# Position bias and causal mask of the softmax heads: added by VectorE, in place of a product on TensorE

## The chip, the cores and the metric

The kernel runs on one core of one Trainium2 chip. The metric is the device time of one execution in microseconds (us). The kernel before has a median of 721.65 us over 3 runs (721.18 to 724.95).

## What is computed

The reference is one layer of a decoder trunk, run for a prompt of 512 tokens and for 8 short samples of 4 tokens with a cache of 256. One input projection feeds three groups of heads: 6 softmax heads with a linear position bias (ALiBi), 6 stick-breaking heads, and a gated MLP over chunks. An output projection, a layer norm, an MLP of width 4096 and a second layer norm follow. The change touches the softmax heads of the prompt alone. Cut to that:

```python
s = jnp.einsum('bhqd,bhnsd->bhqns', qc, kg).astype(jnp.float32) * scale
dist = (pc[:, None, None] - kpos).astype(jnp.float32)
s = s - slopes[:, None, None, None] * dist
mask = ok[..., None] & (kpos <= pc[:, None, None])
s = jnp.where(mask, s, -jnp.inf)
p = jax.nn.softmax(s.reshape(Bn, H, qb, ns * MOBA_BLOCK), axis=-1)
...
return jnp.einsum('bhqns,bhqnsd->bhqd', p, vg)
```

With 512 tokens, key blocks of 256 and three blocks to choose, every past block is chosen, so that this is plain causal softmax attention with a bias of slope times (key position minus query position).

## The kernel before, in words

The kernel is written engine by engine. Each engine has its own program in a fixed order, and semaphores join them: `pe.wait_ge(x, n)` holds everything behind it on TensorE until semaphore `x` has reached `n`. Nothing is scheduled by a planner.

**Products in three passes.** An fp32 matrix is split into a high and a low part in the type fp32r (`w_hi`, `w_lo`, `h_hi`, `h_lo`), and each product is done as high by high, low by high, high by low. All such products stand on line 1510. The input projection has 22 units of 128 output columns. A unit is cut into 8 chunks of 6 matmuls each (`in_unit(u, c)`); chunks 0 to 3 are 256 columns wide and chunks 4 to 7 are 288.

**The attention loop.** The two kinds of prompt heads are handled as 48 items: item n is head pair i = n // 8, query block t = (n % 8) // 2 and head h = n % 2, with L = 128 (t + 1) keys. Items 0 to 23 are softmax heads, 24 to 47 are stick-breaking heads. So L is 128, 128, 256, 256, 384, 384, 512, 512 through the 8 items of a pair. The chunks of units 3 to 21 are woven in. TensorE does in step n: `scores(n)`, a chunk, `turn_probs(n - 2)`, a chunk, at every fourth step `values`, in the first three steps of a pair `turn_kv`, and a third chunk.

- `scores(n)` (lines 1541 to 1563) writes one of the two score banks `s_bank` in PSUM. For a softmax item it is three accumulated matmuls of L columns: the bias and mask (L1557: the scaled identity `sid_r` by the table of distances `dist_r`, which holds -1e30 beyond the diagonal), and two for query by key (L1558, L1559). It first waits until the bank is free (`p_written`, n - 1).
- `row_max(n)` on VectorE (L1114, L1116): the maximum of each row of the bank, then its negative, `nmx`.
- `probs(n)` on ScalarE (L788): exp of the bank with `nmx` as bias and the row sum as a second output, into `prob`.
- `normalise(n - 1)` on VectorE (L1123, L1125) comes behind `row_max(n)` in VectorE's order: `prob` times the inverse row sum. It releases `p_scaled`.
- `turn_probs(n)` on TensorE (L1572) waits for `p_scaled` and transposes `prob`.

VectorE and ScalarE carry more work in the same fixed order. VectorE (lines 1144 to 1169): in step s = n % 8 behind `normalise`, a copy `kv_new` (s = 2, L1155), the low part of the finished head pair `m_lo` (s = 3, L1159), half of each projected unit (`read_half`, s = 2, 5, 7, L1080, L1082), and the low parts of the stacked queries and keys of the next pair (`stack_q_lo`, s = 0 and 4, L1092; `stack_k_lo`, s = 6, L1099). ScalarE (lines 800 to 834) does the other halves, the high parts of these stacks (L756, L763), the copies of keys and values `k_tok` and `v_tok` (L810), the high part of the finished pair (L817), and `w_hi` of the next weights (L692). So a query stack goes ScalarE, then VectorE, and what stands behind it on VectorE waits for both.

**GpSimd** computes the low parts of all weights (L582), and early on writes `dist_r` (L599), the six scaled identities `sid_r` (L601), `id_r` and `below_r` (L603, L604). TensorE waits for all nine (`bias_ready`, H + 3) before item 0.

Of the kernel before, what the change touches and what calls it, by code (L numbers as in the profile page):

```python
# [27 lines left out]
ALU = mybir.AluOpType  # L28
ACT = mybir.ActivationFunctionType
AX_X = mybir.AxisListType.X  # L30
F32 = mybir.dt.float32
F32R = mybir.dt.float32r
I32 = mybir.dt.int32

P = 128
D_MODEL = 1024
KT = D_MODEL // P
SEQ = 512
# [9 lines left out]
H = 6  # L48
PAIRS = H // 2
# [14 lines left out]
SLOPES = [0.25, 0.0625, 0.015625, 0.00390625, 0.5, 0.125]  # L64
# [40 lines left out]
def hybrid_layer(nc, x_prompt, x_sample, weights, cache_k_a, cache_v_a, cache_k_b, cache_v_b,  # L105
# [14 lines left out]
    with ExitStack() as ctx:  # L120
        def sb(name, shape, dt=F32, to=None):
            return (to or ctx).enter_context(nc.sbuf_tensor(name, shape, dt))

        def sem(name):
            return ctx.enter_context(nc.semaphore(name))
# [13 lines left out]
        warm = sb("warm", [P, 1])  # L139
        qbd = [sb(f"qbd{y}", [P, NB, PAIRS, 32]) for y in range(2)]  # L140
        dist_r = sb("dist_r", [P, SEQ], F32R)
        sid_r = sb("sid_r", [P, H, P], F32R)
        id_r = sb("id_r", [P, P], F32R)
        below_r = sb("below_r", [P, P], F32R)

# [29 lines left out]
        prob = sb("prob", [P, 3, SEQ], to=pr)  # L175
        prob_t = [sb(f"prob_t{h}", [P, QT * (QT + 1) // 2, P], to=pr) for h in range(2)]
        mx = sb("mx", [P, 2], to=pr)
        nmx = sb("nmx", [P, 2], to=pr)
# [4 lines left out]
        keep = sb("keep", [P, 2, SEQ], to=pr)  # L183
# [57 lines left out]
        def c_(name, r=P, lo=0, hi=None):  # L241
            where, t = (CONST, cst) if name in CONST else (S_CONST, s_cst)
            at, n = where[name]
            if t is s_cst and at < S_ROWS:
                t = s_rows
            elif t is s_cst:
                at -= S_ROWS
            return t[0:r, at + lo:at + (n if hi is None else hi)]
# [35 lines left out]
        kv_out = [sem(f"kv_out{j}") for j in range(2)]  # L284
        s_ready = sem("s_ready")
        row_maxed, max_ready = sem("row_maxed"), sem("max_ready")
        p_written = sem("p_written")
        rsum_inverted = sem("rsum_inverted")
        stick_left = sem("stick_left")
# [287 lines left out]
        def _(pool):  # L577
# [19 lines left out]
            lo_part(2, 2 % STAGE, 2)  # L597
            pool.wait_ge(const2_loaded, 32)
            pool.tensor_copy(dist_r[:, :], dist[:, :]).then_inc(bias_ready, 1)  # L599
            for h in range(H):  # L600
                pool.tensor_scalar(sid_r[:, h, :], c_("ident"), SLOPES[h], None, ALU.mult).then_inc(bias_ready, 1)  # L601
            lo_part(3, 3 % STAGE, 3)
            pool.tensor_copy(id_r[:, :], c_("ident")).then_inc(bias_ready, 1)  # L603
            pool.tensor_copy(below_r[:, :], c_("below_neg")).then_inc(bias_ready, 1)  # L604
# [82 lines left out]
        def _(act):  # L687
# [87 lines left out]
            def probs(n):  # L775

                i, s, t, h, L = item(n)
                b = n % 2
                if i < PAIRS:
                    act.wait_ge(max_ready, n + 1)  # L780
                else:
                    act.wait_ge(s_ready, n + 1)
                    act.wait_ge(p_scaled, n - 1)
                    act.activation(keep[:, b, 0:L], s_bank[b][:, 0:L], ACT.Sigmoid, scale=-1.0)
                if n >= 3:
                    act.wait_ge(pt_ready, n - 2)
                if i < PAIRS:
                    act.activation(prob[:, n % 3, 0:L], s_bank[b][:, 0:L], ACT.Exp, bias=nmx[:, b:b + 1],  # L788
                                   accum_out=rsum[:, b:b + 1]).then_inc(p_written, 1)
                else:  # L790
                    act.activation(prob[:, n % 3, 0:L], s_bank[b][:, 0:L], ACT.Sigmoid).then_inc(p_written, 1)
# [8 lines left out]
            for n in range(ITEMS + 4):  # L800
                i, s = divmod(n, 8)
# [221 lines left out]
        def _(dve):  # L1023
# [85 lines left out]
            def row_max(n):  # L1109

                i, s, t, h, L = item(n)
                b = n % 2
                dve.wait_ge(s_ready, n + 1)
                dve.tensor_reduce(mx[:, b:b + 1], s_bank[b][:, 0:L], AX_X, ALU.max).then_inc(row_maxed, 1)  # L1114
                dve.wait_ge(row_maxed, n + 1)
                dve.tensor_scalar(nmx[:, b:b + 1], mx[:, b:b + 1], -1.0, None, ALU.mult).then_inc(max_ready, 1)  # L1116

# [23 lines left out]
                                  ALU.mult).then_inc(p_scaled, 1)  # L1141

            dve.wait_ge(const2_loaded, 32)
            for n in range(ITEMS + 4):
                i, s = divmod(n, 8)
                if n < 8 * PAIRS:
                    row_max(n)
                if 1 <= n <= 8 * PAIRS:
                    normalise(n - 1)
                elif 8 * PAIRS < n <= ITEMS:  # L1150
                    stick(n - 1)
                if n < ITEMS and s == 2:
                    y, p = divmod(i, PAIRS)
                    dve.wait_ge(kv_turned, 3 * i + 3)
                    dve.tensor_copy(kv_new[y][:, :, P * p:P * (p + 1)],  # L1155
                                    acc[0:NS, 3, 0:2 * P].rearrange("t (w c) -> t w c", w=2)).then_inc(kv_new_ready, 1)
                if i >= 1 and s == 3:
                    dve.wait_ge(mhi_ready, i)
                    dve.scalar_tensor_tensor(m_lo[:, i - 1, PROMPT], o_bank[:, :], 1 / ALPHA,  # L1159
                                             m_hi[:, i - 1, PROMPT].bitcast(F32), ALU.mult,  # L1160
                                             ALU.subtract).then_inc(m_ready, 1)
                if i and n < ITEMS and s == 0:
                    stack_q_lo(i, 1)
                if n < ITEMS and s in (2, 5, 7):
                    read_half(3 * (i + 1) + (2, 5, 7).index(s))
                if i + 1 < 2 * PAIRS and s == 4:
                    stack_q_lo(i + 1, 0)
                if i + 1 < 2 * PAIRS and s == 6:
                    stack_k_lo(i + 1)
# [309 lines left out]
        def _(pe):  # L1479
# [50 lines left out]
            for u in range(3):  # L1530
                for c in range(8):
# [4 lines left out]
                    if u == 0 and c == 0:  # L1536
                        turn_x(6)
                        turn_x(7)
            pe.wait_ge(bias_ready, H + 3)

            def scores(n):

                i, s, t, h, L = item(n)
                b = n % 2
                if n >= 2:
                    pe.wait_ge(p_written, n - 1)
                if s == 0:
                    pe.wait_ge(k_stack_hi, 2 * (i + 1))
                    pe.wait_ge(k_stack_lo, 2 * (i + 1))
                if s in (0, 4):  # L1550
                    pe.wait_ge(q_stack_hi, 8 * i + 4 * (s // 4 + 1))
                    pe.wait_ge(q_stack_lo, 8 * i + 4 * (s // 4 + 1))
                out = s_bank[b]
                q = q_st[:, h, :, P * t:P * (t + 1)]
                k = k_st(i)[:, h, 0:L]
                if i < PAIRS:
                    pe.matmul(out[:, 0:L], sid_r[:, 2 * i + h, :], dist_r[:, SEQ - L:SEQ], start=True, stop=False)  # L1557
                    pe.matmul(out[:, 0:L], q[:, 0, :], k, start=False, stop=False)  # L1558
                    pe.matmul(out[:, 0:L], q[:, 1, :], k, start=False, stop=True).then_inc(s_ready, 1)  # L1559
                else:  # L1560
                    pe.matmul(out[:, 0:L], q[:, 0, :], k, start=True, stop=False)
                    pe.matmul(out[:, 0:L], q[:, 1, :], k, start=False, stop=False)  # L1562
                    pe.matmul(out[:, L - P:L], id_r[:, :], below_r[:, :], start=False, stop=True).then_inc(s_ready, 1)
# [431 lines left out]
```

## Time and profile before

| | |
|---|---|
| median of 3 runs | 721.65 us (721.18 to 724.95) |
| the profiled execution, its own time | 721.94 us |
| its span in the trace | 720.1 us |
| mean granted TensorE clock | 0.986 of full speed |
| TensorE matmul busy | 679.5 us (94% of the span) |
| VectorE busy | 375.7 us (52%) |
| ScalarE busy | 265.6 us (37%) |
| GpSimd busy | 356.5 us (50%) |

The profiled execution is 0.29 us above the median, and 1.8 us of its time lie outside the span. The softmax items run from about 46 to 126 us of the span, the stick-breaking items from there to 212 us. Behind them come the samples, the output projection and the MLP. Busy shares are averages over stages with different limits, so the next step is to look at the stretch from 46 to 126 us by itself.

### The profile page before, as it was taken

How to read it: one execution, taken by the hardware profiler on the slowest of the kernel's cores; microseconds unless marked ns; L12 is line 12 of the kernel's file. 1: busy time of each engine (PE TensorE's matmuls, PEld its weight loads, DVE VectorE, ACT ScalarE, POOL GpSimd, SP SyncE). 2: the span in 40 equal slices, each digit the busy share in tenths (PEclk: the TensorE clock that was granted, in tenths of full speed). 3: DMA queues.
4: the chain of work that ended last, by engine and by line, in shares of the span. 5: the costliest groups of instructions: out<-in, count | busy, mean ns of one | idle time of the engine just before them, and what ended most of it. 6: DMA issues, size and time to landing. Idle time of an engine off the chain costs nothing.

```text
span 720.1 us, 14217 instructions
## 1 busy us (share of the span) xinstructions
PE 679.5 (94%) x5574; PEld 655.7 (91%) x5574; DVE 375.7 (52%) x691; ACT 265.6 (37%) x493; POOL 356.5 (50%) x452
## 2 busy tenths in 40 slices
PE   2999999999998699989999999999999999999993
PEld 1789999999997379989999999999999999999992
DVE  5556465576654445879742543623525436235247
ACT  5465666677656233643221212212112122121112
POOL 2973333444446205436954555545545555455417
PEclk9999999999999899999999999999999999999998
DMA  5244321222446933200332222222222222222303
GB/s 212 88 139 145 101 65 56 89 73 74 133 137 204 319 124 117 88 30 10 138 118 88 73 103 67 89 96 78 95 87 74 92 83 87 89 86 87 117 1 124
DMA packets 32961, 73.42 MB, mean 102 GB/s; under 512 B 3666, under 2 KB 18546, under 8 KB 32914
## 3 DMA queue, kind: packets, MB, share of 16 engines
q1 hardware_dynamic: 25778, 68.73, 28.2%
q10 hardware_dynamic: 6576, 3.38, 1.6%
q0 software_dynamic: 560, 0.66, 0.5%
q8 instruction: 32, 0.52, 0.3%
q14 instruction: 15, 0.12, 0.1%
HBM read 67.15 MB, written 5.60 MB: 101 GB/s over the span
## 4 chain that ended last, share of the span: by engine, by line
PE 85%; DVE 5%; DMA 2%; POOL 2%; issue 2%; SPq 2%; ACT 1%; DVEq 0%; POOLq 0%
PE acc L1510 74%; PE o_bank L1586 2%; DMA k_t<-cache_k_b 2%; POOL w_lo L582 1%; POOL res L662 1%; PE t_bank L1572 1%; PE acc L1572 1%; DMA xin<-x_prompt 1%; PE acc L1602 1%; SPq L481 1%; PE t_bank L1685 1%; SPq L511 1%; PE s_bank L1562 1%; DVE x_st L1038 1%; PE acc L1489 1%
## 5 line engine op out<-in xcount | busy, mean ns | idle before, releaser
L582 POOL TENSOR_TENSOR w_lo<-w_raw,w_hi 128x256 fp32r<-128x256 f32 x360 | 288.7, 832 | 292.7 <-ACT w_hi L692 292.6
L1510 PE MATMUL acc<-h_hi,w_hi 128*128 128x256 f32 (+1 forms) x864 | 258.7, 299 | 3.1 <-DVE h_lo L1053 1.7
L1510 PE MATMUL acc<-h_lo,w_hi 128*128 128x256 f32 (+1 forms) x864 | 250.9, 290 | 0.0
L1510 PE MATMUL acc<-h_hi,w_lo 128*128 128x256 f32 (+1 forms) x864 | 250.5, 290 | 0.0
L692 ACT ACTIVATE w_hi<-w_raw 128x1024 fp32r<-128x1024 f32 x90 | 95.2, 1059 | 246.9 <-PE acc L1510 224.2
L1510 PEld LDWEIGHTS acc<-h_hi,w_hi 128*128 128x128 f32 x864 | 164.6, 191 | 6.1 <-issue 4.3
L1510 PE MATMUL acc<-m_hi,w_lo 128*128 128x256 f32 (+1 forms) x576 | 166.4, 289 | 0.0
L1510 PE MATMUL acc<-m_lo,w_hi 128*128 128x256 f32 (+1 forms) x576 | 166.4, 289 | 0.0
L1510 PE MATMUL acc<-m_hi,w_hi 128*128 128x256 f32 (+1 forms) x576 | 166.1, 288 | 0.0
L1510 PEld LDWEIGHTS acc<-h_lo,w_hi 128*128 128x128 f32 x864 | 164.7, 191 | 0.4
L1510 PEld LDWEIGHTS acc<-h_hi,w_lo 128*128 128x128 f32 x864 | 164.0, 190 | 0.0
L1510 PEld LDWEIGHTS acc<-m_hi,w_hi 128*128 128x128 f32 x576 | 108.8, 189 | 0.1
L1510 PEld LDWEIGHTS acc<-m_lo,w_hi 128*128 128x128 f32 x576 | 108.6, 189 | 0.0
L1510 PEld LDWEIGHTS acc<-m_hi,w_lo 128*128 128x128 f32 x576 | 108.2, 188 | 0.0
L1434 DVE TENSOR_TENSOR res<-res,acc 128x256 f32<-128x256 f32 x112 | 48.3, 436 | 101.0 <-PE acc L1510 101.0
L1423 DVE TENSOR_SCALAR relu<-acc 128x288 f32<-128x288 f32 x28 | 12.8, 457 | 88.1 <-PE acc L1510 88.1
L1360 DVE TENSOR_TENSOR m_lo<-hid,m_hi 128x544 fp32r<-128x544 f32 (+2 forms) x36 | 38.0, 1056 | 1.2
L1092 DVE TENSOR_TENSOR q_st<-z_q,q_st 64x256 fp32r<-64x256 f32 x48 | 22.8, 475 | 24.4 <-ACT q_st L756 23.3
L1358 DVE CAST m_hi<-hid 128x544 fp32r<-128x544 f32 (+2 forms) x36 | 31.4, 872 | 1.2
L996 ACT ACTIVATE relu<-acc 128x256 f32<-128x256 f32 x28 | 10.7, 383 | 44.1 <-PE acc L1510 44.1
L1356 DVE TENSOR_TENSOR hid<-relu 128x544 f32<-128x544 f32 (+2 forms) x36 | 25.4, 704 | 1.2
L652 POOL TENSOR_TENSOR wo_lo<-w_raw,wo_hi 128x1024 fp32r<-128x1024 f32 x4 | 9.7, 2445 | 26.6 <-ACT wo_hi L907 26.6
(239 smaller groups left out, 787.1 us busy)
## 6 DMA issues: line engine op xcount, KB each, us to landing
w_raw<-weights SPq DMA_DIRECT2D x94, 512.0 KB, 3.2
k_t<-cache_k_a SPq DMA_DIRECT2D x16, 192.0 KB, 3.2
k_t<-cache_k_b SPq DMA_DIRECT2D x16, 192.0 KB, 6.0
xin<-x_prompt SPq DMA_DIRECT2D x4, 512.0 KB, 5.6
y_prompt<-y_n SPq DMA_DIRECT2D x8, 256.0 KB, 2.0
v_pg<-cache_v_a SPq DMA_DIRECT2D x8, 192.0 KB, 4.3
v_pg<-cache_v_b SPq DMA_DIRECT2D x8, 192.0 KB, 6.5
k_t<-cache_v_b SPq DMA_DIRECT2D x8, 192.0 KB, 4.0
```

Source lines behind the costliest of these rows:

```text
L582: op = pool.tensor_tensor(w_lo[:, slot, part], w_raw[:, stage, part], w_hi[:, slot, part].bitcast(F32), ALU.subtract)
L692: act.activation(w_hi[:, slot, :], w_raw[:, stage, :], ACT.Copy).then_inc(hi_done, 1)
L996: act.activation(relu[:, j, halves(0)], acc[:, 2 * (j % 2), 0:WIDE[0]], ACT.Relu).then_inc(acc_act, 1)
L1092: dve.tensor_tensor(q_st[OWN[1 - (h ^ order)], h, order, cols], z, hi, ALU.subtract).then_inc(q_stack_lo, 1)
L1356: dve.tensor_tensor(hid[:, j % 2, cols], relu[:, j, cols], relu[:, j, cols], ALU.mult).then_inc(sq_sem, 1)
L1358: dve.tensor_copy(m_hi[:, FG * par + j, cols], hid[:, j % 2, cols]).then_inc(hi_sem, 1)
L1360: return dve.tensor_tensor(m_lo[:, FG * par + j, cols], hid[:, j % 2, cols], m_hi[:, FG * par + j, cols].bitcast(F32), ALU.subtract)
L1423: dve.tensor_scalar(relu[:, j, halves(1)], acc[:, 2 * (j % 2) + 1, 0:WIDE[1]], 0.0, None, ALU.max).then_inc(acc_dve, 1)
L1434: dve.tensor_tensor(res[:, m, halves(hf)], res[:, m, halves(hf)], acc[:, 2 * (m % 2) + hf, 0:WIDE[hf]], ALU.add).then_inc(acc_dve, 1)
L1510: mm = pe.matmul(out, w[:, slot, cols(k)], x[:, ks[k], halves(hf)], start=(fresh and k == 0 and pas == 0), stop=last)
L1572: mm = pe.transpose(pt_bank(n)[:, P * kb:P * (kb + 1)], prob[:, n % 3, P * kb:P * (kb + 1)], ident(P))
L1586: mm = pe.matmul(o_bank[r, P * t:P * (t + 1)], v_tok[i % 2][:, kb, r], prob_t[hh][:, t * (t + 1) // 2 + kb, :], start=(kb == 0), stop=(kb ...
```

## The change

The matmul of L1557 goes. TensorE writes query by key alone, and VectorE computes `keep = slope * dist_r + s_bank` in one `scalar_tensor_tensor` for each item, from the bank into the SBUF tile `keep`. This tile exists already, for the stick-breaking items. The maximum and the exp read `keep` in place of the bank. The bank is free for `scores(n + 2)` once this one instruction is done (`biased`), and no longer only after the exp. The tile `sid_r`, its six GpSimd instructions and their part of the wait go too.

```diff
-        sid_r = sb("sid_r", [P, H, P], F32R)
...
+        biased = sem("biased")
...
-            for h in range(H):
-                pool.tensor_scalar(sid_r[:, h, :], c_("ident"), SLOPES[h], None, ALU.mult).then_inc(bias_ready, 1)
...
                 if i < PAIRS:
-                    act.activation(prob[:, n % 3, 0:L], s_bank[b][:, 0:L], ACT.Exp, bias=nmx[:, b:b + 1],
+                    act.activation(prob[:, n % 3, 0:L], keep[:, b, 0:L], ACT.Exp, bias=nmx[:, b:b + 1],
                                    accum_out=rsum[:, b:b + 1]).then_inc(p_written, 1)
...
                 dve.wait_ge(s_ready, n + 1)
-                dve.tensor_reduce(mx[:, b:b + 1], s_bank[b][:, 0:L], AX_X, ALU.max).then_inc(row_maxed, 1)
+                if n >= 2:
+                    dve.wait_ge(p_written, n - 1)
+                dve.scalar_tensor_tensor(keep[:, b, 0:L], dist_r[:, SEQ - L:SEQ].bitcast(F32), SLOPES[2 * i + h],
+                                         s_bank[b][:, 0:L], ALU.mult, ALU.add).then_inc(biased, 1)
+                dve.wait_ge(biased, n + 1)
+                dve.tensor_reduce(mx[:, b:b + 1], keep[:, b, 0:L], AX_X, ALU.max).then_inc(row_maxed, 1)
                 dve.wait_ge(row_maxed, n + 1)
...
             dve.wait_ge(const2_loaded, 32)
+            dve.wait_ge(bias_ready, 3)
...
-            pe.wait_ge(bias_ready, H + 3)
+            pe.wait_ge(bias_ready, 3)
...
                 if n >= 2:
-                    pe.wait_ge(p_written, n - 1)
+                    pe.wait_ge(biased if n - 2 < 8 * PAIRS else p_written, n - 1)
...
                 if i < PAIRS:
-                    pe.matmul(out[:, 0:L], sid_r[:, 2 * i + h, :], dist_r[:, SEQ - L:SEQ], start=True, stop=False)
-                    pe.matmul(out[:, 0:L], q[:, 0, :], k, start=False, stop=False)
+                    pe.matmul(out[:, 0:L], q[:, 0, :], k, start=True, stop=False)
                     pe.matmul(out[:, 0:L], q[:, 1, :], k, start=False, stop=True).then_inc(s_ready, 1)
```

What stands on TensorE around `scores(13)`, first before, then with the change (the line numbers of the changed kernel are a few lower or higher: its L1514 is L1510 here, its L1575 is L1572):

```order
L1510 MATMUL acc<-h_hi,w_lo 128x288
L1557 MATMUL s_bank<-dist_r,sid_r 128x384 [waits p_written]
L1558 MATMUL s_bank<-m_lo,q_st 128x384
L1559 MATMUL s_bank<-m_lo,q_st 128x384
L1510 MATMUL acc<-h_hi,w_hi 128x288
```

```order
L1514 MATMUL acc<-h_hi,w_lo 128x288
L1561 MATMUL s_bank<-m_lo,q_st 128x384 [waits biased]
L1562 MATMUL s_bank<-m_lo,q_st 128x384
L1514 MATMUL acc<-h_hi,w_hi 128x288
```

One matmul of three has gone, and the wait is for VectorE in place of ScalarE.

What stands on VectorE from `m_lo` to the release of item 12's probabilities, before:

```order
L1159 SCALAR_TENSOR_TENSOR m_lo<-o_bank,m_hi 128x512 [waits mhi_ready]
L1114 TENSOR_REDUCE mx<-s_bank 128x1 [waits s_ready]
L1116 TENSOR_SCALAR nmx<-mx 128x1 [waits row_maxed]
L1123 RECIPROCAL rinv<-rsum 128x1 [waits p_written]
L1125 TENSOR_SCALAR prob<-prob,rinv 128x256 [waits rsum_inverted]
L1092 TENSOR_TENSOR q_st<-z_q,q_st 64x256 [waits q_stack_hi]
L1092 TENSOR_TENSOR q_st<-z_q,q_st 64x256
L1092 TENSOR_TENSOR q_st<-z_q,q_st 64x256 [waits q_stack_hi]
L1092 TENSOR_TENSOR q_st<-z_q,q_st 64x256
L1114 TENSOR_REDUCE mx<-s_bank 128x1 [waits s_ready]
L1116 TENSOR_SCALAR nmx<-mx 128x1 [waits row_maxed]
L1123 RECIPROCAL rinv<-rsum 128x1 [waits p_written]
L1125 TENSOR_SCALAR prob<-prob,rinv 128x384 [waits rsum_inverted]
```

With the change, from the second `row_max` of these (item 13) on:

```order
L1114 SCALAR_TENSOR_TENSOR keep<-dist_r,s_bank 128x384 [waits p_written,s_ready]
L1117 TENSOR_REDUCE mx<-keep 128x1 [waits biased]
L1119 TENSOR_SCALAR nmx<-mx 128x1 [waits row_maxed]
L1126 RECIPROCAL rinv<-rsum 128x1 [waits p_written]
L1128 TENSOR_SCALAR prob<-prob,rinv 128x384 [waits rsum_inverted]
```

Each `row_max` has one instruction more ahead of it, and nothing else has moved.

## Rows read from the trace of the kernel before

**Rows 1.** Windows: busy us of each engine in two stretches (count), clock, DMA.

```profile
46.00:126.00 80.00, 78.38 (x659) 75.79 (x658) 46.66 (x133) 50.58 (x124) 30.61 (x48) 1.00 0.32 100
126.00:212.00 86.00, 86.00 (x741) 83.43 (x740) 53.44 (x94) 57.35 (x128) 34.89 (x45) 1.00 0.29 93
```

**Rows 2.** Timeline of TensorE, score matmuls of each width: start, us, engine, line.

```profile
46.26 0.27 PE L1558 MATMUL s_bank<-m_hi,q_st 128*128 128x128 f32 x1
46.36 0.28 PE L1559 MATMUL s_bank<-m_hi,q_st 128*128 128x128 f32 x1
...
54.13 0.28 PE L1558 MATMUL s_bank<-m_hi,q_st 128*128 128x256 f32 x1
54.25 0.28 PE L1559 MATMUL s_bank<-m_hi,q_st 128*128 128x256 f32 x1
...
87.66 0.33 PE L1558 MATMUL s_bank<-m_lo,q_st 128*128 128x384 f32 x1
87.83 0.34 PE L1559 MATMUL s_bank<-m_lo,q_st 128*128 128x384 f32 x1
...
93.80 0.39 PE L1558 MATMUL s_bank<-m_lo,q_st 128*128 128x512 f32 x1
94.03 0.39 PE L1559 MATMUL s_bank<-m_lo,q_st 128*128 128x512 f32 x1
```

**Rows 3.** Groups by form, 46 to 128 us, VectorE: busy us, mean ns, idle before.

```profile
L1114 DVE TENSOR_REDUCE mx<-s_bank 128x1 f32<-128x512 f32 x6 | 4.1, 685 | 2.2 <-PE s_bank L1559 2.2
...
L1114 DVE TENSOR_REDUCE mx<-s_bank 128x1 f32<-128x384 f32 x6 | 3.3, 558 | 1.8 <-PE s_bank L1559 1.7
...
L1114 DVE TENSOR_REDUCE mx<-s_bank 128x1 f32<-128x256 f32 x6 | 2.5, 423 | 2.7 <-PE s_bank L1559 2.7
...
L1114 DVE TENSOR_REDUCE mx<-s_bank 128x1 f32<-128x128 f32 x6 | 1.7, 286 | 0.1
```

**Rows 4.** All instructions of lines 1159 and 1211: ns min/median/max.

```profile
L1159 DVE SCALAR_TENSOR_TENSOR m_lo<-o_bank,m_hi x6: 691/692/692, 87.3 to 221.2; 128x512 fp32r<-128x512 f32 x6
...
L1211 DVE TENSOR_REDUCE v_s<-vsq x1: 1486/1486/1486, 230.8 to 230.8; 128x20 f32<-128x1280 f32 x1
```

**Rows 5.** Groups by form, 46 to 128 us, ScalarE.

```profile
L756 ACT ACTIVATE q_st<-z_q 64x256 fp32r<-64x256 f32 x24 | 9.9, 413 | 0.4
...
L744 ACT ACTIVATE z_kv<-acc 128x256 f32<-128x256 f32 x6 | 2.3, 385 | 1.6 <-PE acc L1510 1.6
```

**Rows 6.** Timeline: TensorE's first weight load behind its wait for `k_tok`.

```profile
52.72 0.42 PEld L1602 LDWEIGHTS acc<-cst,z_kv 128*128 128x128 f32 x4 [1.85 <-ACT k_tok L810]
```

**Rows 7.** Timeline, VectorE and TensorE's weight load: item 8.

```profile
78.10 1.77 DVE L1092 TENSOR_TENSOR q_st<-z_q,q_st 64x256 fp32r<-64x256 f32 x4 [3.19 <-ACT q_st L756]
...
80.50 0.29 DVE L1125 TENSOR_SCALAR prob<-prob,rinv 128x128 f32<-128x128 f32 x1
...
81.14 0.14 PEld L1572 LDWEIGHTS t_bank<-cst,prob 128*128 128x128 f32 x1
```

**Rows 8.** Timeline, VectorE and TensorE's weight load: items 11 and 12.

```profile
87.32 0.69 DVE L1159 SCALAR_TENSOR_TENSOR m_lo<-o_bank,m_hi 128x512 fp32r<-128x512 f32 x1 [0.70 <-ACT m_hi L817]
88.21 0.56 DVE L1114 TENSOR_REDUCE mx<-s_bank 128x1 f32<-128x384 f32 x1 [0.19 <-PE s_bank L1559]
...
92.92 0.42 DVE L1125 TENSOR_SCALAR prob<-prob,rinv 128x384 f32<-128x384 f32 x1
...
94.86 0.36 PEld L1572 LDWEIGHTS t_bank<-cst,prob 128*128 128x128 f32 x3
```

**Rows 9.** Timeline, VectorE and TensorE's weight load: item 14.

```profile
94.46 0.69 DVE L1114 TENSOR_REDUCE mx<-s_bank 128x1 f32<-128x512 f32 x1 [0.75 <-PE s_bank L1559]
...
100.00 0.49 DVE L1125 TENSOR_SCALAR prob<-prob,rinv 128x512 f32<-128x512 f32 x1
...
102.16 0.36 PEld L1572 LDWEIGHTS t_bank<-cst,prob 128*128 128x128 f32 x3
```

**Rows 10.** Timeline, VectorE: the query stack ahead of item 0.

```profile
47.79 3.39 DVE L1092 TENSOR_TENSOR q_st<-z_q,q_st 64x256 fp32r<-64x256 f32 x4 [0.94 <-ACT q_st L756]
```

## Prediction

> **What bounds the kernel now.** I read the windows first. From 46 to 126 us, where the softmax items run, TensorE is busy 78.4 of 80 us at full clock, and from 126 to 212 us all 86 of 86; VectorE and ScalarE are busy 47 and 51 of the first 80 [rows 1]. So TensorE sets the pace, and a matmul taken from it is worth its full step. What it idles is nearly all one wait, for ScalarE's copy `k_tok` at 52.72 us [rows 6]. But VectorE and ScalarE work for each other in turn, in a fixed order, and busy shares don't tell how late they may be. For that I read the margins: from the end of `normalise(n)` (L1125) to the weight load of `turn_probs(n)` (L1572), item by item. Three in a pair of heads are short. Item 8: 81.14 - 80.79 = 0.35 us [rows 7]. Item 12: 94.86 - 93.34 = 1.52 us [rows 8]. Item 14: 102.16 - 100.49 = 1.67 us [rows 9]. Items 16, 20 and 22 of the third pair and items 4 and 6 of the first repeat these to some hundredths, so there are eight such places. The other sixteen margins are 1.8 us or more, and only one or two additions lie ahead of them. What counts is what the change does to these eight.
>
> **What TensorE saves.** One matmul goes from each of 24 items. Its price is the step from one score matmul's start to the next: 0.10, 0.12, 0.17 and 0.23 us at 128, 256, 384 and 512 columns [rows 2]. Six items have each width: 6 x 0.62 = 3.7 us. By their own durations (0.27 to 0.39 us) they would be worth twice that, but matmuls overlap, so the step is the right price. Nothing else lies beside them, since TensorE is full.
>
> **What VectorE gains in work.** The new instruction reads PSUM and SBUF and writes SBUF, with one scalar. Line 1159 is the same kind: 691 to 692 ns at 512 columns in all six cases [rows 4], and the maximum over as many columns takes 685 [rows 3]. I therefore price it like the maximum at each width: 0.29, 0.42, 0.56, 0.69 us [rows 3]. The maximum must wait for it on the same engine, and `nmx` starts 0.03 to 0.04 us behind the maximum for the same reason. So each `row_max` ends later by D = 0.33, 0.46, 0.60, 0.73 us. That is 6 x 2.12 = 12.7 us on VectorE, which has 33 us of idle time here; only its place matters.
>
> The maximum now reads SBUF. Line 1211 does that: 1280 columns in 1486 ns [rows 4], which is the 685 ns of 512 PSUM columns plus 768 at 1.04 ns, the step between the widths in [rows 3]. So it costs the same. The Trainium skill (VectorE: DVE Perf Modes, section on the TRN2 errata) gives VectorE 58 cycles of fixed cost from SBUF against 120 from PSUM; that would take some 65 ns off each maximum, which these rows don't show. By it the sum at the end would be about 1.1 us lower.
>
> The exp on ScalarE reads SBUF too. A copy of 256 columns takes 413 ns from SBUF and 385 from PSUM [rows 5]: bounds 0 to 0.03 us each. I take 0 and keep 17 x 0.03 = 0.5 us for the range.
>
> **The eight waits, worked for the pair of items 8 to 15.** I move along two engines and compare how much later VectorE ends with how much earlier TensorE arrives.
>
> Item 8. Ahead of `normalise(8)` on VectorE stand the query stack, which waits for ScalarE and through it for TensorE [rows 7], and `row_max(9)`. It is later by D(128) = 0.33. TensorE comes earlier by the matmuls of items 9 and 10: 0.22. Wait: 0.33 + 0.22 - 0.35 = 0.20 us.
>
> Item 12. `row_max(11)` makes exp(11) later by 0.46, ScalarE then the high part of the finished pair, VectorE then `m_lo` (L1159). That ends at 88.01 + 0.46 = 88.47, and `row_max(12)`, which began at 88.21, begins 0.26 late. It adds 0.60; exp(12), the query stack on both engines and `row_max(13)` follow in one chain, with 0.60 more. `normalise(12)` is late by 1.46. TensorE is early by items 12, 13, 14: 0.17 + 0.17 + 0.23 = 0.57. Wait: 1.46 + 0.57 - 1.52 = 0.51 us.
>
> Item 14. VectorE had been free 0.75 us when `row_max(14)` began [rows 9], so of 1.46 late 0.71 is left. `row_max(14)`, exp(14), the key stack and `row_max(15)` are again one chain: 0.71 + 0.73 + 0.73 = 2.17 late. TensorE is early by items 12 to 16, 0.90, less the 0.51 just waited: 0.39. Wait: 2.17 + 0.39 - 1.67 = 0.89 us.
>
> The pair: 0.20 + 0.51 + 0.89 = 1.60 us lost, 1.24 saved, +0.36. The third pair is the same, +0.36.
>
> First pair. The wait for `k_tok` hangs on a fixed time before item 0, by way of the query stack and `row_max(0)`. It ends 0.33 us later, and the 0.20 us saved on items 0 and 1 go into it. At item 4 there is no `m_lo` ahead: 0.60 + 0.60 late, 0.17 + 0.23 early, wait 0.08. Item 6: 1.20 - 0.75 + 1.46 = 1.91 late, 0.73 - 0.08 = 0.65 early, wait 0.89. Lost 0.33 + 0.08 + 0.89 = 1.30; saved on items 2 to 7 1.04; +0.26.
>
> **Edits at nothing.** The bank is released earlier, but `scores(n)` never waited for it: TensorE stands without idle time, apart from [rows 6]. The new wait for `p_written` ahead of each addition is met, as `normalise` in the step before has waited for the same count. GpSimd's six instructions stand ahead of the low part of unit 3, which TensorE needs only behind `scores(0)`; its three units of projection before that are the cover. Without it, what the six take would be a gain. From 126 to 212 us nothing changes and TensorE is full, so a shift passes through. What follows hangs on the end of that stretch.
>
> **Sum.** 0.26 + 0.36 + 0.36 = +1.0 us on the profiled execution's 721.94, or 722.9. The median is 0.29 lower, so I predict 722.6 us. Nearly all of a saving of 3.7 us, and 1 us more, goes into new waits: 1.30 + 1.60 + 1.60 = 4.5, and the 0.2 that items 0 and 1 lose.
>
> **Rivals.**
>
> *The waits stay away.* If VectorE's lateness is covered (margins measured too small, or an addition that is shorter than the row), only the first wait moves: -3.7 + 0.2 + 0.33 = -3.2, 718.5 us. For it: VectorE and ScalarE are both 40% idle. Against: that idle time lies in waits for TensorE that the chain of each pair uses up. Chance 0.07.
>
> *The reduction is shorter from SBUF.* 17 of the 24 additions lie on a chain above (5, 6, 6), so each 0.05 us less for the pair of addition and maximum takes 0.85 us off. At 0.065: 721.5 us. For it is the skill's rule above; against it line 1211. Chance 0.12.
>
> *The addition costs more in SBUF (slower).* Instructions with two SBUF inputs take longer beside GpSimd: four of L1092 need 3.39 us at 47.79 [rows 10], where GpSimd works, and 1.77 at 78.10 [rows 7], where it doesn't. GpSimd is busy 30.6 of these 80 us [rows 1]. If the addition (mean 0.49 us) doubled in that share, it would be 0.19 longer on average: 17 x 0.19 = +3.2, 725.8 us. It decides from 0.16 us more for each addition (+2.7, with the 1.0 above). Against: the addition has one SBUF input, and L1159 never left 692 ns. Chance 0.13.
>
> *The clock falls.* New waits of up to 0.9 us could lower the granted clock. Against: it stood at 1.00 through the whole stretch with a wait of 1.85 us in it [rows 1, 6]. Chance 0.03, some 2 us more.
>
> My forecast, small losses and savings that nearly cancel: 0.65.
>
> **Range.** Each of the nine places may be off by 0.25 us (the restart behind a wait is in it), which is 2.2; with the exp's 0.5 on top the forecast's own range is 720.4 to 725.3. To hold 8 in 10 I go from 719.6, between the first two rivals, to 726.2, past the third. A measurement here can tell 0.5% (3.6 us) from no change. Faster by more than that needs more than the whole saving: 0.05. Slower needs 725.3: the third rival, the fourth with a bad sum, and the top of my own range: 0.15. Same: 0.80.
>
> **What would show it.** Right: 24 additions at 0.29 to 0.69 us; TensorE idle in front of L1572 at items 4, 6, 8, 12, 14, 16, 20 and 22, most (0.9 us) at 6, 14 and 22, with VectorE's L1125 as releaser; some 4.5 us of TensorE idle time more in the stretch; item 24 starting about 1 us later. Wrong: no idle time at L1572 (first rival), additions of two lengths, the longer beside GpSimd (third), a maximum below 0.62 us at 512 columns (second), or a clock below 1.00. The prediction also fails if ScalarE, delayed with VectorE, holds TensorE at a projection unit, which I take to have margins of an item or more.

## The result, and the profile after

The median is 725.26 us against 722.31 us, 22 runs each: ratio 1.0041, 95% interval 1.0031 to 1.005. One of the 22 executions of the kernel before took 843.26 us; the ratio goes by the fast runs alone, without it. The change costs 3 us: clear of no change by the interval, and a little less than the 0.5% that I had called the limit of telling. The profiled execution has a span of 723.9 us, 3.8 more than before, at a mean clock of 0.987 against 0.986.

The windows of the changed kernel, as in [rows 1] (busy us of TensorE, its weight loads, VectorE, ScalarE and GpSimd, with counts; clock; DMA share and GB/s):

```profile
46.00:126.00 80.00, 74.70 (x621) 71.11 (x621) 56.71 (x152) 48.04 (x118) 26.73 (x43) 1.00 0.31 100
126.00:212.00 86.00, 84.74 (x732) 81.61 (x730) 55.71 (x98) 58.24 (x131) 37.50 (x49) 1.00 0.27 84
```

TensorE had 1.6 us without work in both stretches together and now has 6.6, at full clock: 5.0 us more, where some 4.5 were forecast. VectorE has 10 us more work in the first. The additions and maxima by form (46 to 130 us; busy us, mean ns, idle before), which answer to [rows 3]:

```profile
L1117 DVE TENSOR_REDUCE mx<-keep 128x1 f32<-128x512 f32 x5 | 3.4, 686 | 0.2
L1114 DVE SCALAR_TENSOR_TENSOR keep<-dist_r,s_bank 128x512 f32<-128x512 f32 x5 | 3.4, 682 | 0.1
...
L1114 DVE SCALAR_TENSOR_TENSOR keep<-dist_r,s_bank 128x384 f32<-128x384 f32 x6 | 3.3, 551 | 1.1 <-PE s_bank L1562 1.0
...
L1114 DVE SCALAR_TENSOR_TENSOR keep<-dist_r,s_bank 128x256 f32<-128x256 f32 x6 | 2.5, 418 | 2.2 <-PE s_bank L1562 2.2
...
L1114 DVE SCALAR_TENSOR_TENSOR keep<-dist_r,s_bank 128x128 f32<-128x128 f32 x6 | 1.7, 283 | 0.1
```

Both are what the sum had: 0.28 to 0.68 us for the addition, and a maximum from SBUF that takes what it took from PSUM (686 and 685 ns). The 58 cycles against 120 of the Trainium skill (VectorE: DVE Perf Modes, section on the TRN2 errata) are not shown here for this instruction.

The weight loads that waited for probabilities or for `k_tok`, in order of time (start, us, line, idle and its releaser), of the changed kernel:

```profile
53.20 0.20 PEld L1605 LDWEIGHTS acc<-cst,z_kv 128*128 128x128 f32 x2 [2.44 <-ACT k_tok L808]
...
74.72 0.42 PEld L1575 LDWEIGHTS t_bank<-cst,prob 128*128 128x128 f32 x4 [0.85 <-DVE prob L1128]
...
82.05 0.14 PEld L1575 LDWEIGHTS t_bank<-cst,prob 128*128 128x128 f32 x1 [0.64 <-DVE prob L1128]
...
95.52 0.31 PEld L1575 LDWEIGHTS t_bank<-cst,prob 128*128 128x128 f32 x3 [0.47 <-DVE prob L1128]
...
103.45 0.31 PEld L1575 LDWEIGHTS t_bank<-cst,prob 128*128 128x128 f32 x3 [0.94 <-DVE prob L1128]
...
111.14 0.14 PEld L1575 LDWEIGHTS t_bank<-cst,prob 128*128 128x128 f32 x1 [0.99 <-DVE prob L1128]
...
124.63 0.31 PEld L1575 LDWEIGHTS t_bank<-cst,prob 128*128 128x128 f32 x3 [0.47 <-DVE prob L1128]
...
132.56 0.20 PEld L1575 LDWEIGHTS t_bank<-cst,prob 128*128 128x128 f32 x2 [0.84 <-DVE prob L1128]
...
140.32 0.14 PEld L1575 LDWEIGHTS t_bank<-cst,prob 128*128 128x128 f32 x1 [0.86 <-DVE prob L1143]
```

Behind the first wait these are items 6, 8, 12, 14, 16, 20, 22 and 24. Seven stand where the forecast had them. L1143 releases item 24, the first stick-breaking item, where it had none.

To compare them with the forecast I take, at each place, how far the start of the score matmuls moved between the two traces, plus the step saved there. In us:

| place | forecast | measured |
|---|---|---|
| first wait, and what items 0 and 1 saved | 0.53 | 0.60 |
| item 4 | 0.08 | 0.10 |
| item 6 | 0.89 | 0.83 |
| item 8 | 0.20 | 0.62 |
| item 12 | 0.51 | 0.48 |
| item 14 | 0.89 | 0.93 |
| item 16 | 0.20 | 0.99 |
| item 20 | 0.51 | 0.48 |
| item 22 | 0.89 | 0.84 |
| item 24 | none | 0.85 |
| sum | 4.7 | 6.7 |

Less the 3.7 saved that is +3.0, against +1.0 forecast. The second score matmul of the last item started at 208.70 us before; in the timeline of the changed kernel:

```profile
212.00 0.39 PE L1565 MATMUL s_bank<-m_lo,q_st 128*128 128x512 f32 x1
```

That is 3.3 us later, and so it is from item 27 on. Of the 0.3 between the two, 0.12 was there before the first item (TensorE's matmuls at 44 us start that much later in this trace), and 0.1 is the step of item 8, where taking the matmul out saved nothing: from the matmul ahead of its scores to the one behind them it is 0.41 us, as before (0.42). The restart behind each wait, 0.04 to 0.06 us, is in the measured column. Another 0.4 comes behind 212 us; I didn't follow it.

**Item 16 (and 8).** The timeline of GpSimd and VectorE in the changed kernel:

```profile
76.32 2.83 POOL L582 TENSOR_TENSOR w_lo<-w_raw,w_hi 128x256 fp32r<-128x256 f32 x4 [5.14 <-ACT w_hi L690]
78.55 2.23 DVE L1090 TENSOR_TENSOR q_st<-z_q,q_st 64x256 fp32r<-64x256 f32 x4 [2.22 <-ACT q_st L754]
...
105.06 2.82 POOL L582 TENSOR_TENSOR w_lo<-w_raw,w_hi 128x256 fp32r<-128x256 f32 x4 [5.15 <-ACT w_hi L690]
107.28 2.59 DVE L1090 TENSOR_TENSOR q_st<-z_q,q_st 64x256 fp32r<-64x256 f32 x4 [2.22 <-ACT q_st L754]
107.82 0.87 POOL L625 CAST sb_r<-s_rows 128x576 fp32r<-128x576 f32 x1
```

In the kernel before, GpSimd was done ahead of the stack:

```profile
74.61 2.97 POOL L582 TENSOR_TENSOR w_lo<-w_raw,w_hi 128x256 fp32r<-128x256 f32 x4 [4.69 <-ACT w_hi L692]
```

The query stack took 1.77 us at 78.10 then [rows 7], GpSimd's low part of the weights having ended at 77.58. ScalarE is now later, so `w_hi` is, so the low part is, and its last 0.60 us lie beside the query stack. At item 16 GpSimd's copy into `sb_r` (L625) follows at once and lies beside it too: there the first two of the stack's four instructions are long (0.88 and 0.77 us for 0.42), at item 8 only the first (0.87). That is 0.46 and 0.82 us more on the chain that ends in `normalise(8)` and `normalise(16)`.

**Item 24.** ScalarE's timeline there, in the changed kernel:

```profile
131.94 0.72 ACT L786 ACTIVATE prob<-keep,nmx 128x512 f32<-128x512 f32 x1 [2.83 <-DVE nmx L1119]
...
133.04 1.05 ACT L690 ACTIVATE w_hi<-w_raw 128x1024 fp32r<-128x1024 f32 x1
134.10 1.28 ACT L782 ACT_TABLE_LOAD   x1
135.40 0.28 ACT L782 ACTIVATE keep<-s_bank 128x128 f32<-128x128 f32 x1
```

Behind exp(23) it has a high part of weights and a table load ahead of item 24. Before, it idled 0.33 us for TensorE ahead of that high part. Now it comes too late to wait for anything, and its lateness reaches TensorE by way of `stick(24)`.

### The profile page after: what moved, and what is told of

Its sections match the earlier page's. It is cut to its first block, busy times and chain, and to the rows that moved or that the text cites. A ratio compares the mean times of both kernels' runs of the same rounds, so it can differ in the third digit from the quotient of the medians.

```text
span 723.9 us, 14209 instructions
## 1 busy us (share of the span) xinstructions
PE 680.9 (94%) x5550; PEld 653.9 (90%) x5550; DVE 388.7 (54%) x715; ACT 265.6 (37%) x493; POOL 352.2 (49%) x446
## 4 chain that ended last, share of the span: by engine, by line
PE 78%; DVE 11%; ACT 4%; issue 3%; DMA 2%; POOL 1%; SPq 1%; ACTq 0%; DVEq 0%
PE acc L1514 68%; DVE q_st L1090 2%; PE o_bank L1589 2%; DMA k_t<-cache_k_b 1%; DVE mx L1117 1%; DVE keep L1114 1%; PE t_bank L1688 1%; POOL res L660 1%; DMA xin<-x_prompt 1%; PE t_bank L1575 1%; DVE x_st L1036 1%; PE acc L1493 1%; ACT prob L786 1%; DVE y_n L1399 0%; DVE res L1289 0%
## 5 line engine op out<-in xcount | busy, mean ns | idle before, releaser
L1514 PE MATMUL acc<-h_hi,w_hi 128*128 128x256 f32 (+1 forms) x864 | 259.3, 300 | 2.8 <-POOL w_lo L582 1.2
L1514 PE MATMUL acc<-h_lo,w_hi 128*128 128x256 f32 (+1 forms) x864 | 250.7, 290 | 0.0
L1514 PE MATMUL acc<-h_hi,w_lo 128*128 128x256 f32 (+1 forms) x864 | 250.5, 290 | 0.0
L1514 PEld LDWEIGHTS acc<-h_hi,w_hi 128*128 128x128 f32 x864 | 164.8, 191 | 6.1 <-issue 3.7
L1514 PE MATMUL acc<-m_hi,w_lo 128*128 128x256 f32 (+1 forms) x576 | 166.4, 289 | 0.0
L1514 PE MATMUL acc<-m_lo,w_hi 128*128 128x256 f32 (+1 forms) x576 | 166.4, 289 | 0.0
L1514 PE MATMUL acc<-m_hi,w_hi 128*128 128x256 f32 (+1 forms) x576 | 166.1, 288 | 0.0
L1514 PEld LDWEIGHTS acc<-h_lo,w_hi 128*128 128x128 f32 x864 | 164.7, 191 | 0.4
L1514 PEld LDWEIGHTS acc<-h_hi,w_lo 128*128 128x128 f32 x864 | 163.9, 190 | 0.0
L1514 PEld LDWEIGHTS acc<-m_hi,w_hi 128*128 128x128 f32 x576 | 108.8, 189 | 0.1
L1514 PEld LDWEIGHTS acc<-m_lo,w_hi 128*128 128x128 f32 x576 | 108.6, 189 | 0.0
L1514 PEld LDWEIGHTS acc<-m_hi,w_lo 128*128 128x128 f32 x576 | 108.2, 188 | 0.0
L1090 DVE TENSOR_TENSOR q_st<-z_q,q_st 64x256 fp32r<-64x256 f32 x48 | 24.7, 514 | 20.6 <-ACT q_st L754 19.5
L786 ACT ACTIVATE prob<-keep,nmx 128x128 f32<-128x128 f32 (+3 forms) x24 | 13.5, 562 | 31.6 <-DVE nmx L1119 31.1
```

The costliest lines, as they stand in the source:

```text
L786: act.activation(prob[:, n % 3, 0:L], keep[:, b, 0:L], ACT.Exp, bias=nmx[:, b:b + 1], accum_out=rsum[:, b:b + 1]).then_inc(p_written, 1)
L1090: dve.tensor_tensor(q_st[OWN[1 - (h ^ order)], h, order, cols], z, hi, ALU.subtract).then_inc(q_stack_lo, 1)
L1514: mm = pe.matmul(out, w[:, slot, cols(k)], x[:, ks[k], halves(hf)], start=(fresh and k == 0 and pas == 0), stop=last)
```

## The experiments

The kernel before, run beside each set, had a median of 722.00 or 722.01 us in all three. Where waits are given they are those between 46 and 212 us (who waited, tile and line, for whom: us in total, times, longest), and shifts are of the score matmuls' start. Item 0 starts up to 2.1 us earlier or 1.1 later than in the trace of the kernel before, so where it says "from 43 us" the shift is less the one that the projection at 43 us already had.

**One half alone: TensorE's.** The kernel before without the bias matmul, and nothing in its place. It leaves the position bias and the mask out of these 24 items.

```diff
-                    pe.matmul(out[:, 0:L], sid_r[:, 2 * i + h, :], dist_r[:, SEQ - L:SEQ], start=True, stop=False)
-                    pe.matmul(out[:, 0:L], q[:, 0, :], k, start=False, stop=False)
+                    pe.matmul(out[:, 0:L], q[:, 0, :], k, start=True, stop=False)
```

> The kernel before without the bias matmul, and nothing put in its place: the softmax heads have neither bias nor mask. VectorE and ScalarE work as before. If a matmul is worth its step (0.10 to 0.23 us) and the margins of before hold (the shortest is 0.35 us, and TensorE comes 0.22 us earlier to it), the time falls by 3.7 us, to a ratio of 0.995, and TensorE never waits at the transposes. If matmuls were worth their own durations it would be 7 us (0.990). If TensorE were not the pace of this stretch, 0.

718.12 us, ratio 0.9957 (0.994 to 0.9974). The scores end 3.25 us earlier, with no wait at a transpose and only the first one left:

```profile
PEld acc L1601 <- ACT k_tok L810: 2.1, 1, 2.1
```

From 43 us it is 3.45. TensorE's idle time there grew by 0.24. So the saving is the matmul's step, 3.7 us less 0.24, and not its duration, which would have given twice that.

**The other half alone: VectorE's.** TensorE keeps the bias; VectorE passes the scores through the same instruction with slope 0 (the edit is shown against the changed kernel).

```diff
-                dve.scalar_tensor_tensor(keep[:, b, 0:L], dist_r[:, SEQ - L:SEQ].bitcast(F32), SLOPES[2 * i + h],
+                dve.scalar_tensor_tensor(keep[:, b, 0:L], dist_r[:, SEQ - L:SEQ].bitcast(F32), 0.0,
...
-                    pe.matmul(out[:, 0:L], q[:, 0, :], k, start=True, stop=False)
+                    pe.matmul(out[:, 0:L], sid_r[:, 2 * i + h, :], dist_r[:, SEQ - L:SEQ], start=True, stop=False)
+                    pe.matmul(out[:, 0:L], q[:, 0, :], k, start=False, stop=False)
```

> The other half alone: TensorE keeps the bias matmul, and VectorE passes the finished scores through the same added instruction (slope 0), with maximum and exp reading the tile. If the loss is a matter of chains against margins, the halves don't add up: TensorE isn't earlier, so the waits at items 4, 12 and 20 stay away, those at 6, 14 and 22 are 0.2 to 0.5 us, the first wait is 0.33 longer, and items 8, 16 and 24 give what the collision with GpSimd and the late table load are worth (0.3 to 0.8 each): +2.5 to +3.5 us in all, ratio 1.004. If the halves added up, this would be the measured change less the first half, 3.0 + 3.7 = +6.7 us (1.009).

725.45 us, ratio 1.0055 (1.0036 to 1.0074), and in the waits:

```profile
PEld t_bank L1579 <- DVE prob L1131: 2.6, 5, 0.8
```

That is 4.0 us, a little over the 2.5 to 3.5 expected. By the ratios the halves are -0.43% and +0.55%, whose sum is +0.12%; together they cost 0.41%, which the intervals alone barely tell apart. The traces are plainer: from 43 us the last scores are 3.45 us earlier with one half and 3.76 later with the other, +0.3 in sum, and 3.18 later with both. They don't add. Whatever TensorE saves while VectorE is late it spends at the next transpose, where it arrives earlier: 5.2 us over seven places with both, 2.6 over five with this half.

**GpSimd kept away from the query stack.** The low part of units 9 and 12 starts behind VectorE's query stack.

```diff
+                if u in (9, 12):
+                    pool.wait_ge(q_stack_lo, 8 * (u // 3 - 1))
```

> The changed kernel, with GpSimd's low parts of units 9 and 12 held back until VectorE is done with the query stacks that they now run beside (items 9 and 17). If GpSimd is what stretches these stacks from 1.77 to 2.23 and 2.59 us, they are 1.77 again, the waits at items 8 and 16 shrink by 0.46 and 0.82, and the time falls by 1.3 us against the changed kernel: ratio to before 1.002. If the stacks are late for another reason (ScalarE), nothing changes: 1.004.

724.55 us, ratio 1.0039 (1.0025 to 1.0052), which is no gain over the changed kernel's 1.0041, where 1.3 us were expected. VectorE's timeline at the same two places, the query stack and `normalise` behind it:

```profile
80.16 1.77 DVE L1092 TENSOR_TENSOR q_st<-z_q,q_st 64x256 fp32r<-64x256 f32 x4 [2.21 <-ACT q_st L756]
...
82.86 0.66 DVE L1130 TENSOR_SCALAR prob<-prob,rinv 128x128 f32<-128x128 f32 x1
...
108.81 1.77 DVE L1092 TENSOR_TENSOR q_st<-z_q,q_st 64x256 fp32r<-64x256 f32 x4 [2.22 <-ACT q_st L756]
...
111.52 0.66 DVE L1130 TENSOR_SCALAR prob<-prob,rinv 128x128 f32<-128x128 f32 x1
```

Both query stacks are back at 1.77 us, so GpSimd was the cause of their length. But GpSimd's low part now lies on `normalise(8)` and `normalise(16)`, which take 0.66 us where they took 0.29 [rows 7]. Less 0.46 and plus 0.37 at item 8, less 0.82 and plus 0.37 at item 16: TensorE's waits fall from 0.62 to 0.55 and from 0.99 to 0.53, about as these give. The contention was moved, not taken away. And behind the first wait the windows show a loss of another kind:

```profile
50.00:54.00 4.00, 1.79 (x13) 1.55 (x12) 3.03 (x10) 1.81 (x5) 1.06 (x2) 0.91 0.17 67
54.00:58.00 4.00, 4.00 (x23) 4.00 (x22) 1.35 (x5) 1.84 (x7) 0.00 (x0) 0.66 0.66 178
```

TensorE stood 2.2 us in the first; in the second it was busy throughout but did 23 matmuls. In the changed kernel the same stretch has 34 at full clock:

```profile
54.00:58.00 4.00, 4.00 (x34) 3.95 (x34) 2.34 (x8) 2.74 (x8) 0.18 (x1) 1.00 0.60 160
```

Part of that stretch ran at the lower of the two levels (1.2 and not 2.4 GHz). By item 4 the scores are 1.6 us later than in the changed kernel, both taken from their item 0.

**Order on VectorE.** `normalise(n - 1)` ahead of `row_max(n)`.

```diff
-                if n < 8 * PAIRS:
-                    row_max(n)
                 if 1 <= n <= 8 * PAIRS:
                     normalise(n - 1)
...
+                if n < 8 * PAIRS:
+                    row_max(n)
```

> The changed kernel, with normalise(n - 1) ahead of row_max(n) in VectorE's order. If the waits at the transposes come from the addition and the maximum of the next item standing ahead of the scaling, those at items 4, 6, 12, 14, 20 and 22 go (measured 0.10, 0.84, 0.48, 0.94, 0.48, 0.84) and those at 8 and 16 shrink by about 0.7 each; the first wait (0.59) and item 24 (0.85) stay. That is -5 us against the changed kernel, ratio to before 0.997. If VectorE is short of time as such, the order changes nothing: 1.004.

730.21 us, ratio 1.0117 (1.0092 to 1.0142): 5.5 us slower than the changed kernel, where 5 us less were expected. The waits from 46 to 150 us (total, times, longest):

```profile
ACT prob L786 <- DVE nmx L1119: 37.6, 20, 3.0
...
DVE rinv L1126 <- ACT prob L786: 5.7, 11, 0.7
PEld o_bank L1589 <- ACT prob_t L795: 4.1, 4, 1.3
```

In the changed kernel the first of these is 31.1 over 19, and the other two are under 0.5 us. VectorE now stands for exp(n - 1) with the scores of item n ready, and ScalarE starts each exp later. What I had taken for two instructions in the wrong order is the overlap that keeps the two engines going.

**The addition twice.** The same instruction once more, into a tile that nobody reads here.

```diff
+                dve.scalar_tensor_tensor(left[:, b, 0:L], dist_r[:, SEQ - L:SEQ].bitcast(F32), SLOPES[2 * i + h],
+                                         s_bank[b][:, 0:L], ALU.mult, ALU.add)
```

> The changed kernel with the addition done twice for each softmax item, the first time into a tile that nobody reads. If 17 of the 24 additions lie on chains that TensorE waits for, and a further instruction without a wait costs its duration less 0.07 us (0.42 on average over the widths), the time rises by 2.4 + 2.8 + 2.8 = 8 us, to a ratio of 1.015 against before, with the rise at the same transposes. If the idle time of VectorE (about 25 of 80 us left) took it up, it would rise by little.

731.73 us, ratio 1.0138 (1.0117 to 1.0159), 0.97% over the changed kernel or 7.0 us, of the 8 expected. In this profile the clock fell behind the first wait, too (0.64 from 52 to 56 us), so not all of it need be the addition. The waits at the transposes are 5.9 us longer than the changed kernel's 5.2; VectorE's idle time does not take the second addition up:

```profile
PEld t_bank L1577 <- DVE prob L1130: 11.1, 8, 1.7
```

**Transposes later.** `turn_probs(n - 2)` one chunk of projection later in each step n as far as 27.

```diff
-                for uc in fill[3 * n:3 * n + 1]:
+                late = n < 8 * PAIRS + 4
+                for uc in fill[3 * n:3 * n + (2 if late else 1)]:
...
```

> The changed kernel with turn_probs(n - 2) one chunk (0.7 to 0.8 us) later in TensorE's order up to item 25: behind the second chunk of step n in place of the first. Nothing in the order of VectorE and ScalarE changes. If the loss is the margin at the transposes, each of the ten waits but the first shrinks by up to 0.8 us: 5 us less, ratio to before 0.997. Against it: ScalarE copies the transposes in step n and may now wait for them, which makes it late in turn, as normalise first did; then the waits come back elsewhere and the ratio stays near 1.004.

725.31 us, ratio 1.0036 (1.002 to 1.0051): no gain clear of noise, where 5 us were expected. From 43 us the last scores are 2.3 us later than in the kernel before, in place of 3.2. The waits moved:

```profile
PEld t_bank L1575 <- DVE prob L1128: 1.9, 4, 0.9
PEld o_bank L1589 <- ACT prob_t L795: 1.9, 4, 0.8
```

The transposes wait 3.3 us less, and the product behind them, which needs ScalarE's copy of the transposed tile, waits 1.9 in place of 0.3. TensorE's weight loads now also stand 0.5 us ahead of the scores at 102.2 and at 131.3 us, which they don't in the changed kernel. So most of what the transposes gain is waited for elsewhere.

**The first maximum ahead.** `row_max(0)` before the second query stack, whose place is then item 0's step.

```diff
-            stack_q_lo(0, 1)
...
-                if i and n < ITEMS and s == 0:
+                if n < ITEMS and s == 0:
```

> The changed kernel with the first maximum ahead of the low parts of the second query stack of pair 0 (on VectorE, stack_q_lo(0, 1) behind row_max(0) in place of ahead of it). The first wait hangs on that order: VectorE starts row_max(0) at 51.3 us, 4 us behind the scores. If so, the wait of 2.2 us falls to some 0.5, and the time by 1.7 us: ratio to before 1.002. If this wait is also what lets the clock fall in some executions (in the trace of the run with the late GpSimd parts it is at 0.66 from 54 to 58 us, which cost 1.2 us), the median gains up to 1 us more.

722.73 us, ratio 1.0004 (0.9992 to 1.0017). TensorE's first wait is 0.6 us in place of 2.2:

```profile
PE acc L1604 <- ACT k_tok L808: 0.6, 1, 0.6
```

That is 1.6 us, and the ratio is 0.37% lower, 2.7 us. The rest would fit a clock that falls in some executions behind a 2.2 us wait, at 1.5 to 1.6 us each in the profiles where it fell, but it wasn't measured apart, and 1.1 us is within the two intervals.

**ScalarE relieved ahead of item 24.** The high part of unit 15 goes behind `v_tok` of item 25.

```diff
+                    if n == 8 * PAIRS + 1:
+                        hi_unit(3 * PAIRS + 2 + RING)
...
-                        hi_unit(u + RING)
+                        if n != 8 * PAIRS - 1:
+                            hi_unit(u + RING)
```

> The changed kernel with ScalarE's high part of unit 15 moved from in front of item 24 to behind the copy of its values. If the wait of 0.85 us at item 24's transpose comes from ScalarE being late there, with its table load of 1.28 us, that wait goes: -0.85 us, ratio to before 1.003. If it comes from VectorE, nothing changes: 1.004.

723.60 us, ratio 1.0029 (1.0015 to 1.0043), less than the changed kernel by what was expected, but within the intervals. ScalarE's timeline:

```profile
132.55 1.28 ACT L782 ACT_TABLE_LOAD   x1
133.84 0.28 ACT L782 ACTIVATE keep<-s_bank 128x128 f32<-128x128 f32 x1
```

This trace started item 0 2.1 us earlier, and the clock fell behind its first wait (0.58 from 52 to 56 us, which cost 1.5 us by item 4), so the times are compared from the transposes of item 22, at 131.95 us here and 132.56 in the changed kernel. From there the first stick item starts 0.95 us earlier, about the 1.05 of the high part. The wait at item 24 is gone: from item 25 on the shift against the kernel before no longer grows, where in the changed kernel it grew by another 0.86 us.

**A choice of items.** The 14 items with n % 8 in 0, 2, 3, 5, 7 (not item 0) go to VectorE, the rest keep TensorE's product.

```diff
+        ON_DVE = [n for n in range(8 * PAIRS) if n % 8 in (0, 2, 3, 5, 7) and n > 0]
```

> The addition on VectorE only for the 14 softmax items whose margins can bear it (steps 0, 2, 3, 5 and 7 of each pair, without item 0); the other 10 keep their bias matmul. The steps of the 14 matmuls are 0.64 + 0.74 + 0.74 = 2.1 us. By the chains nobody waits for the additions: item 12's chain is late by 0.26 + 0.60 against a margin of 1.52 less 0.17, item 14's by 0.11 + 0.73 against 1.67 less 0.50. So -1.4 us (if item 24 still waits for ScalarE) to -2.1 us against before, ratio 0.997 to 0.998. If every addition cost something, as 3.0 us for 24 of them would say, it would be +1.8 us (1.002).

721.16 us, ratio 0.9989 (0.9978 to 1.0001): 0.8 us, less than the 1.4 to 2.1 expected and not quite clear of no change. Two waits for probabilities are left in the stretch, at items 16 and 24, the two that the forecast lacked or had too small:

```profile
PEld t_bank L1591 <- DVE prob L1156: 0.8, 1, 0.8
...
PEld t_bank L1591 <- DVE prob L1141: 0.6, 1, 0.6
```

**What is the repairs' own.** The kernel before with the first maximum ahead (the edit above, nothing else).

> The kernel before with the early first maximum alone (stack_q_lo(0, 1) behind row_max(0)). The wait of 1.6 us for the copy of the keys hangs on the same order there: it falls to some 0.3, -1.3 us, ratio 0.998. That tells how much of the gain of the changed kernel with the same edit is the wait (1.6) and how much the clock.

720.55 us, ratio 0.9981 (0.9969 to 0.9993). That is 1.4 us that need no addition on VectorE. The other two repairs were not tried by themselves in the kernel before; it has no wait at a transpose that they could take away.

**The choice with the three repairs** (first maximum ahead, low part behind the query stack, high part later).

> The additions on VectorE for the same 14 items, with the three repairs that worked: early first maximum, GpSimd's low parts of units 9 and 12 behind the query stacks, ScalarE's high part of unit 15 behind the copy of its values. By the parts: -2.1 - 1.3 = -3.4 us against before, ratio 0.995, with no wait at a transpose.

719.01 us, ratio 0.9959 (0.9942 to 0.9975), below both kernels. Its windows:

```profile
43.00:123.00 80.00, 79.70 (x667) 76.92 (x667) 54.70 (x148) 50.92 (x126) 32.80 (x51) 1.00 0.33 106
123.00:209.00 86.00, 86.00 (x742) 83.51 (x741) 54.95 (x96) 57.58 (x128) 35.58 (x46) 1.00 0.30 93
```

TensorE idles 0.3 us of 166. Of the 3.0 us gained the experiment before has 1.4. The other 1.6 are the choice of items, with the two repairs that it needs; the two intervals overlap a little.

**All 24 with the three repairs.**

> The changed kernel, all 24 items on VectorE, with the three repairs. If they add, 3.0 - 2.5 - 0.5 - 0.85 = -0.9 us against before, ratio 0.999; the six waits at items 6, 12, 14, 20, 22 and 8/16 in their short form stay.

720.45 us, ratio 0.998 (0.9965 to 0.9995), with

```profile
PEld t_bank L1579 <- DVE prob L1132: 4.8, 7, 1.0
```

The repairs take 0.6% off the changed kernel, and the regular waits of each pair stay. By the medians, the move of all 24 is worth nothing against the kernel before with the one repair (0.9981). In the two profiles the last scores, from 43 us, are 0.7 us later with it.

## Why the prediction was right, and where its sum was short

The mechanism was right. The saving of 3.7 us is the matmul's step (the first experiment). The addition costs what L1159 did [rows 4]. The lateness of VectorE and ScalarE runs along the chain of each pair, and TensorE pays at the places named. Seven of the nine places with a forecast are within 0.07 us. The second experiment and the doubled addition show that VectorE's time is paid for although it was 42% idle in the first stretch before, and 29% with the change.

Forecast was +1.0 us on the profiled execution, measured +3.8 on its span and +3.0 on the medians: 725.26 us against 722.6 forecast, at the very top of the forecast's own range (725.3). That range allowed 0.25 us for each place; three places were off by 0.42, 0.79 and 0.85, and they fit in it only because the other seven were nearly exact. That is luck, and not a range well reasoned. Three terms were mis-sized or missing.

- *Item 8, 0.20, measured 0.62, and item 16, 0.20, measured 0.99.* The sum took the third pair for a copy of the second, and moved only VectorE and TensorE. GpSimd moved too, by way of ScalarE, onto the query stack, at item 16 with its copy into `sb_r` as well. The 0.46 and 0.82 that the stack took longer give 0.66 and 1.02 us with the 0.20, for 0.62 and 0.99 measured, and GpSimd behind the stack changed both waits about by what VectorE's rows say.
- *Item 24, none, measured 0.85.* The step that failed is "from 126 to 212 us nothing changes". I had margins for the 24 items that the change touches, and not for the one behind them, where ScalarE passes a high part and a table load. Taking the high part away took the wait away.
- *The rest.* The restarts, 0.04 to 0.06 us at each wait, were in the range and not in the sum; 0.1 us is item 8's step, which wasn't saved; 0.4 us behind 212 us are unexplained. The exp, put at nothing with 0.03 us in the range, took 0.03 more at each width. The seven places, 0.04 us under the forecast in all, show neither that nor the restarts; what offsets them wasn't worked out.

The rivals. That the waits stay away is refuted. So is the shorter reduction. The rival with contention in SBUF named the right mechanism and the wrong instruction: the addition that began at 86.14 us beside GpSimd took 0.42, the one at 81.91 without it 0.41, while the query stack, both of whose inputs are in SBUF, stretched, and so did the scaling of `prob` from SBUF to SBUF once GpSimd was moved onto it. The Trainium skill (SBUF — State Buffer, section "SBUF: two separate sides") lists the first of these: VectorE with two SBUF inputs contends with a GpSimd instruction that reads SBUF. The trace agrees, with 2.23 and 2.59 us for 1.77. The clock rival, at 0.03, was underrated, though the clock stayed at 1.00 in the profile of the changed kernel: my argument, the first wait of the kernel before that left it at 1.00 [rows 1, 6], held for that wait (1.6 us of TensorE's own idle time) and not for one of 2.2.

## What to carry to other kernels

Margins have to be taken for every engine that a shift moves, and for the first items behind the stretch that is changed: the two misses here were a GpSimd instruction and a table load that nobody had edited. Where two engines work for each other in turn, one that is 40% idle still has no free time at the places where its partner waits, and what the bound engine saves is spent at the next of these. Then move only those pieces of work whose margin is larger than the sum of what is added ahead of them, and compare with the same repairs in the kernel before: here 14 of 24 items, with all three repairs, gave some 0.2% on top of the one repair there, all 24 nothing.

## What was not expected of the hardware

- Four VectorE instructions with two SBUF inputs (64x256) took 1.77 us alone, 2.23 with the end of GpSimd's weight work beside them, 2.59 with a copy of GpSimd's behind that, and 3.39 beside GpSimd's work in full [rows 10]. A scaling of 128x128 in SBUF took 0.66 in place of 0.29. GpSimd's low part, which had started first, did not get longer (2.97 us before, 2.82 now); its copy of 128x576, started beside the stack, took 0.87 in place of 0.66.
- TensorE's clock behind a single wait in a busy stretch. In six profiles TensorE stood 2.2 us or more in the first wait (the changed kernel and the experiments with GpSimd late, the order on VectorE, the addition twice, the transposes later and the high part later): the granted clock fell behind it in three (GpSimd late, twice, high part late), to 0.66, 0.64 and 0.58 over the lowest 4 us, and not in the others. In the first and last of these it cost 1.6 and 1.5 us by item 4. In the eight with 2.0 us or less it stayed at 1.00. What decides between the three and the three isn't known.
- The exp took 0.72 us from SBUF at 512 columns and 0.69 from PSUM, 0.03 more as at the other widths, which is the bound of [rows 5].
